# Unread products of TensorE at the end of the expert layers, and the key weights scaled there

## The chip, the cores and the metric

One core of one Trainium2 chip runs the whole program. The metric is the device time of one execution in microseconds, given as the median of three runs. Beside the runs stands one execution that was recorded by the profiler; all durations of single instructions come from it.

## What is computed

The reference runs two blocks of a network over 1024 tokens of width 1024 (the second block puts 16 learned tokens in front, so its first layer has 1040). What matters here is the second block. Its two layers each end in a mixture of 64 experts, and between the two lies latent attention:

```
h = h + short_conv_mixer(rmsnorm(h, ...))
h = h + hier_moe(rmsnorm(h, norm_ffn_g[0]), ...)      # experts, layer 0
a = rmsnorm(h, kv_g) @ w_dkv                          # key latents, 320 columns
cq = rmsnorm(rmsnorm(h, norm_mix_g[1]) @ w_dq, cq_g)  # query latents, 384 columns
... attention with 8 heads ...
h = h + hier_moe(rmsnorm(h, norm_ffn_g[1]), ...)      # experts, layer 1
return rmsnorm(h, final_norm_g)
```

`hier_moe` sends each token to two experts, multiplies their outputs by a gate and adds both to the token's row. All numbers are float32.

## The kernel before

The program is a chain of phases. A phase is a block in which each engine has its own instruction stream, and engines wait for each other through semaphores. At the end of a phase all five engines meet twice: first in the barrier that closes the block (L3363 for the experts, which is the line of `with nc.Block()`; L1924 for the phase ahead of them), then, after GpSimd has cleared the phase's semaphores, in a second barrier at L84. In the first one each engine runs a DRAIN instruction, raises a semaphore, and waits until GpSimd releases all.

`experts` runs twice, for layer 0 and for layer 1. It goes over 32 pairs of experts with weights that SyncE's queue loads three pairs ahead. For the last pair TensorE makes the products with the down weights in `down_half` (L3259); ScalarE and VectorE copy the result out of PSUM, and GpSimd scatters the rows to `ys` in HBM. SyncE waits for the scatters to land (L3403) and then issues the first loads of the next phase, `after.rows(sp)`. Ahead of that it has issued `after.start(sp)`: for layer 0 (`after` is a `LatentLoads`) the gains, the query weights `wq`, the key weights `wk` (L3638, issued at 1575.15 us) and rows of `h`. At the end of its stream ScalarE calls `after.scale_first`, which for layer 0 multiplies the query weights by the gains. A branch on `count` skips the part for experts with more than 64 rows; it is not run with these inputs. For layer 1 `after` is a `FinalLoads`, which only loads.

`combine_and_latents` (names beginning with `cl__`) follows layer 0. For each of nine tiles t of 128 tokens:

- `make(t)` on VectorE (L3606, L3607) adds the two gated expert rows to the row of `h`;
- `roots(t)` on ScalarE (L3848, L3850) takes the root of the mean square, and `scale(t)` on VectorE (L3911, L3915) divides by it;
- `turn(t)` on TensorE (L3766) transposes the tile, `turned_out(t)` on ScalarE (L3858) copies it out;
- `query_products(t)` (L3780) and `key_products(t)` (L3788) on TensorE multiply with `wq` and `wk`;
- ScalarE and VectorE normalise the latents, and TensorE turns them.

The order on each engine is written out by hand. VectorE: make(0), scale(0), make(1), the key weights times their gains (`pre.scale_second`, L3661, eight instructions), scale(1), make(2), scale(2), make(3), then a loop. ScalarE: roots(0), turned_out(0), roots(1), roots(2), roots(3), turned_out(1), and so on. TensorE: turn(0), query_products(0), turn(1), key_products(0), query_products(1).

`combine_out` (names beginning with `co__`) follows layer 1. It makes eight tiles of the output in the same way; VectorE adds the rows of five tiles and TensorE those of three (t = 2, 4, 6), VectorE scales all eight and SyncE stores them. The rows of tiles 0 to 3 are loaded by `after.rows` ahead of the barrier (L3999), those of tiles 4 to 7 behind it (L4034).

The phase ahead of the experts (`back_and_route`) already has unread products of TensorE:

```
def keep_busy(times):

    for i in range(times):
        mm(acc[:, A], ident[:], hnT[:, X[-1] % 2, 0:HK].rearrange("p k q -> p (k q)"), start=True, stop=True)
```

Its last instruction on TensorE is `keep_busy(6)` (L2205): six products of 128 by 128 with 128 by 512 elements that nobody reads, and then the barrier at L1924.

Of the kernel before, what the change touches and what calls it, by code (L numbers as in the profile page):

```python
# [11 lines left out]
P = 128  # L12
# [5 lines left out]
KT = DM // P  # L18
# [1788 lines left out]
QR = 384  # L1807
# [1345 lines left out]
def experts(nc, D, layer, tokens, keep, spill, gate, gu_slots, d_slots, xe, g_loaded, u_loaded, d_loaded, x_loaded, after, within):  # L3153
# [5 lines left out]
    with Phase(nc, "ex", within) as ph:  # L3159
# [121 lines left out]
        def y_second(b):  # L3281
            return nc.vector.tensor_copy(ysb[:, b, 512:], y_ps[:, 1])  # L3282
# [80 lines left out]
        with nc.Block() as block:  # L3363
# [87 lines left out]
            @block.tensor  # L3451
            def _(pe):

                def turn(p):
                    pe.wait_ge(x_loaded[p % 2], 16 * (p // 2 + 1))
                    if p >= 1:
                        pe.wait_ge(m["xT_out"], 2 * p)
                    turn_rows(p % 2).then_inc(m["x_turned"], 1)

                def last_product(p):  # L3460
                    pe.wait_ge(m["hT_out"], p + 1)
                    pe.wait_ge(d_loaded[p % RING], 16 * d_slots[p % RING].pieces * (p // RING + 1))
                    if p >= 1:
                        pe.wait_ge(m["y_out"], 2 * p)
                    down_products(p % 2, d_slots[p % RING].rows).then_inc(m["y_done"], 1)

                turn(0)
                for p in range(PAIRS_M):
                    end = p == PAIRS_M - 1
                    if end:  # L3470
                        last_product(p - 1)
                    pe.wait_ge(m["xT_out"], 2 * (p + 1))
                    pe.wait_ge(g_loaded[p % RING], 16 * (p // RING + 1))
                    gate_products(p % 2, gu_slots[p % RING]).then_inc(m["g_done"], 1)
                    if p >= 1 and not end:
                        last_product(p - 1)
                    pe.wait_ge(u_loaded[p % RING], 16 * (p // RING + 1))
                    up_products(p % 2, gu_slots[p % RING]).then_inc(m["h_done"], 1)
                    if p + 1 < PAIRS_M:
                        turn(p + 1)  # L3480
                    pe.wait_ge(m["h_out"], p + 1)
                    turn_hidden(p % 2).then_inc(m["h_turned"], 1)
                    if p == LOOK:
                        count = spilled(pe)
                pe.wait_ge(m["hT_out"], PAIRS_M)
                pe.wait_ge(m["y_out"], 2 * (PAIRS_M - 1))
                for k in range(2):
                    pe.wait_ge(d_ends[k], 16)
                    last = down_half((PAIRS_M - 1) % 2, d_slots[(PAIRS_M - 1) % RING].rows, k)
                last.then_inc(m["y_done"], 1)  # L3490
                with pe.If(0 < count):
                    spill_products(pe)
                    pe.wait_ge(m["y_out"], 2 * PAIRS_M)
                    for n in ("w_used", "x_used"):
                        pe.sem_inc(s[n], 1)
                    with pe.Fori(0, SPILL_PAIRS) as i:
                        with pe.If(2 * i < count):
                            pe.wait_ge(s["x_loaded"], 16 * i + 16)
                            turn_rows(0).then_inc(s["x_turned"], 1)
                            pe.wait_ge(s["xT_out"], 2 * i + 2)  # L3500
                            pe.wait_ge(s["gu_loaded"], 64 * i + 64)
                            gate_products(0, gu_slots[0]).then_inc(s["g_done"], 1)
                            up_products(0, gu_slots[0]).then_inc(s["h_done"], 1)
                            pe.wait_ge(s["h_out"], i + 1)
                            turn_hidden(0).then_inc(s["h_turned"], 1)
                            pe.wait_ge(s["hT_out"], i + 1)
                            pe.wait_ge(s["d_loaded"], 64 * i + 64)
                            down_products(0, d_slots[0].rows).then_inc(s["y_done"], 1)
                            pe.wait_ge(s["y_out"], 2 * i + 2)
                            for n in ("w_used", "x_used"):  # L3510
                                pe.sem_inc(s[n], 1)
# [47 lines left out]
            @block.vector  # L3559
            def _(dve):  # L3560
                v = Chain(dve, v_own)

                def rows_out(p):
                    dve.wait_ge(m["x_turned"], p + 1)
                    xT_second(p % 2).then_inc(m["xT_out"], 1)

                def y_half(p):
                    if p >= 2:
                        dve.wait_ge(y_stored[p % 2], 16 * (p // 2))
                    dve.wait_ge(m["y_done"], p + 1)  # L3570
                    y_second(p % 2).then_inc(m["y_out"], 1)

                rows_out(0)
                for p in range(PAIRS_M):
                    if p >= 1:
                        y_half(p - 1)
                    dve.wait_ge(m["silu_done"], p + 1)
                    dve.wait_ge(m["h_done"], p + 1)
                    hidden(p % 2).then_inc(m["h_out"], 1)
                    if p + 1 < PAIRS_M:  # L3580
                        rows_out(p + 1)
                    if p == 1:
                        gates(dve, v)
                    if p == 2:
                        spill_plan(dve, v)
                        dve.sem_inc(planned, 1)
                    if p == LOOK:
                        count = spilled(dve)
                y_half(PAIRS_M - 1)
                with dve.If(0 < count):  # L3590
                    spill_slots(dve, Chain(dve, slots_own))
                    with dve.Fori(0, SPILL_PAIRS) as i:
                        with dve.If(2 * i < count):
                            dve.wait_ge(s["x_turned"], i + 1)
                            xT_second(0).then_inc(s["xT_out"], 1)
                            dve.wait_ge(s["silu_done"], i + 1)
                            dve.wait_ge(s["h_done"], i + 1)
                            hidden(0).then_inc(s["h_out"], 1)
                            dve.wait_ge(s["seen"], i + 1)
                            dve.wait_ge(s["y_done"], i + 1)  # L3600
                            y_second(0).then_inc(s["y_out"], 1)


def gathered_sum(nc, v, y, gate, h, out, t):
# [87 lines left out]
def combine_and_latents(nc, D, gate, h_in, h_out, part, pre, cq, ckv, kr, next_loads):  # L3692

    QT, CT, KW = QR // P, KVR // P, KVR + ROPE
    with Phase(nc, "cl") as ph:
# [35 lines left out]
        with nc.Block() as block:  # L3731
# [24 lines left out]
            def _(pe):  # L3756
# [62 lines left out]
                def fold_parts(t):  # L3819
# [3 lines left out]
                    mm(aq[:, b, 0:QR], fold[:], parts[:, 0:QR], start=True, stop=True).then_inc(q_done, 1)  # L3823
                    mm(ak[:, b, 0:KW], fold[:], parts[:, QR:], start=True, stop=True).then_inc(k_done, 1)

                turn(0)
                for t in range(TT - 1):
                    query_products(t)
# [63 lines left out]
            def _(dve):  # L3892
# [53 lines left out]
                make(0)  # L3946
                scale(0)
                make(1)
                pre.scale_second(nc, dve)
                scale(1)  # L3950
                make(2)
                scale(2)
# [15 lines left out]
class FinalLoads:  # L3968
# [24 lines left out]
        sp.dma_start(self.hb[:, t], self.h_in[P * t:P * t + P]).then_inc(self.h_loaded[t], 16)  # L3993

    def scale_first(self, nc, act):
        pass

    def rows_in(self, sp, t):
# [320 lines left out]
```

## Time and profile before

| | us |
|---|---|
| median of 3 runs | 2768.99 |
| lowest and highest run | 2765.22, 2770.50 |
| the profiled execution: its own time | 2772.07 |
| the profiled execution: span from first to last instruction | 2770.4 |

The profiled execution took 1.67 us beside its span. Its mean granted TensorE clock was 0.971 of full speed. TensorE was busy for 2456.0 us of the span (89%), VectorE for 1064.8 (38%), ScalarE for 542.0 (20%), GpSimd for 345.0 (12%). A clock of 1.00 in a row is 2.4 GHz, 0.50 is 1.2 GHz. In the trace one float32 product of TensorE is two records (a weight load and a matmul each); a transpose is one.

### The profile page before, as it was taken

The numbers are of one execution on the slowest core, as the hardware profiler recorded it, in microseconds if no ns is written. First come the engines' busy times: TensorE is split into PE (matmuls) and PEld (weight loads), VectorE is DVE, ScalarE is ACT, GpSimd is POOL, SyncE is SP. The second block draws the span as 40 slices with busy tenths as digits, with TensorE's granted clock in tenths as the row PEclk, the third lists the DMA queues.
The fourth block names the chain that finished last, engine by engine and source line by source line (L and its number), as shares of the span: only waits on it lengthen the run. The fifth ranks groups of instructions, "written<-read, shape, count | busy, mean of one in ns | idle before, by whom it ended". The sixth has DMA issues, their size and how long they took to land. (4 is left out here: it accounts for less than half of the span.)

```text
span 2770.4 us, 39407 instructions
## 1 busy us (share of the span) xinstructions
PE 2456.0 (89%) x16286; PEld 1528.4 (55%) x16286; DVE 1064.8 (38%) x2180; ACT 542.0 (20%) x1226; POOL 345.0 (12%) x365
## 2 busy tenths in 40 slices
PE   9999988898999898997777779999999989787775
PEld 5444568447888554554444355766674545444442
DVE  3473654666555643211111153445545431111114
ACT  1312455210000011111111132322331111111112
POOL 3321002400000211111111000000003011111110
PEclk9999999999999999999999989999999999999998
DMA  3111010231113226999999970000113499999998
GB/s 117 35 38 52 6 48 5 83 110 46 32 45 119 99 107 254 416 425 425 425 426 426 395 296 23 17 25 8 49 48 137 178 379 424 425 426 425 426 424 331
DMA packets 86838, 566.06 MB, mean 204 GB/s; under 512 B 19312, under 2 KB 19472, under 8 KB 56688
## 3 DMA queue, kind: packets, MB, share of 16 engines
q1 hardware_dynamic: 61616, 506.86, 44.9%
q0 software_dynamic: 20144, 38.79, 3.7%
q10 hardware_dynamic: 4896, 17.83, 1.6%
q8 instruction: 133, 2.18, 0.3%
q14 instruction: 49, 0.40, 0.0%
HBM read 529.06 MB, written 65.01 MB: 214 GB/s over the span
## 5 line engine op out<-in xcount | busy, mean ns | idle before, releaser
L3231 PE MATMUL ex__h_ps<-all__arena,ex__xT 128*64 128x256 f32 x3392 | 407.7, 395 | 106.5 <-DMA all__arena<-in_w_up_t 82.2
L3231 PEld LDWEIGHTS ex__h_ps<-all__arena,ex__xT 128*64 128x64 f32 x3392 | 249.8, 142 | 276.5 <-DMA all__arena<-in_w_up_t 121.5
L3282 DVE COPY ex__ysb<-ex__y_ps 128x512 f32<-128x512 f32 x64 | 44.3, 692 | 495.8 <-PE ex__y_ps L3251 485.8
L3251 PE MATMUL ex__y_ps<-b__w,ex__hT 128*64 128x512 f32 x640 | 148.6, 606 | 30.5 <-issue 30.5
L3411 POOL DMA_INDIRECT b__rows<-s_hn,mo__queue x60 | 60.6, 1011 | 749.2 <-PE ex__x_ps L3224 749.2
L3273 DVE TENSOR_TENSOR ex__hs<-ex__sg,ex__h_ps 128x256 f32<-128x256 f32 x64 | 27.0, 422 | 304.5 <-PE ex__h_ps L3231 304.5
L2534 PE MATMUL cm__acc<-all__arena,cw__w 128*128 128x260 f32 x576 | 135.7, 386 | 2.6 <-PEq L84 2.3
L2534 PE MATMUL cm__acc<-all__arena,cm__sums 128*128 128x260 f32 x576 | 134.3, 383 | 0.2 <-DVEq L2610 0.2
L2534 PEld LDWEIGHTS cm__acc<-all__arena,cw__w 128*128 128x128 f32 x576 | 110.4, 192 | 20.4 <-issue 3.3
L2534 PEld LDWEIGHTS cm__acc<-all__arena,cm__sums 128*128 128x128 f32 x576 | 109.3, 190 | 17.4 <-issue 0.6
L3264 ACT COPY ex__xT<-ex__x_ps 128x512 f32<-128x512 f32 x64 | 37.5, 586 | 384.1 <-PE ex__x_ps L3224 384.1
L3251 PEld LDWEIGHTS ex__y_ps<-b__w,ex__hT 128*64 128x64 f32 x640 | 49.6, 139 | 109.4 <-issue 107.1
L2920 PE MATMUL hd__o<-all__arena 128*128 128x128 f32 x704 | 96.4, 282 | 6.4 <-ACT all__arena L2990 6.4
L2920 PEld LDWEIGHTS hd__o<-all__arena 128*128 128x128 f32 x704 | 85.0, 191 | 21.6 <-ACT all__arena L2990 14.9
L3231 PE MATMUL ex__h_ps<-mo__wx,ex__xT 128*64 128x256 f32 x704 | 80.8, 382 | 14.9 <-DMA mo__wx<-in_w_gate_t 7.8
L1955 POOL MEMSET mo__ident<- 128x128 f32 x2 | 0.4, 204 | 736.7 <-POOLq L84 736.7
L3279 ACT COPY ex__ysb<-ex__y_ps 128x512 f32<-128x512 f32 x64 | 37.5, 586 | 260.7 <-PE ex__y_ps L3251 253.0
L3224 PE MATMUL ex__x_ps<-mo__ident,b__rows 128*128 128x128 f32 x512 | 75.8, 292 | 13.6 <-PEq L84 13.6
L2075 PE MATMUL pb__acc<-b__w,all__arena 128*128 128x512 f32 x192 | 86.2, 593 | 1.8 <-PEq L84 1.8
L374 PE MATMUL fr__acc<-X__xT,fr__w 128*128 128x512 f32 x192 | 87.0, 603 | 0.0
L3224 PEld LDWEIGHTS ex__x_ps<-mo__ident,b__rows 128*128 128x128 f32 x512 | 63.3, 195 | 39.1 <-issue 39.1
L3416 POOL DMA_INDIRECT s_ys<-ex__ysb,mo__queue x64 | 64.4, 1006 | 108.7 <-DVE ex__ysb L3282 91.6
(546 smaller groups left out, 4088.8 us busy)
## 6 DMA issues: line engine op xcount, KB each, us to landing
all__arena<-in_w_up_t SPq DMA_DIRECT2D x64, 2048.0 KB, 43.7
all__arena<-in_w_gate_t SPq DMA_DIRECT2D x42, 2048.0 KB, 43.6
b__w<-in_w_down_t SPq DMA_DIRECT2D x40, 2048.0 KB, 44.8
mo__wx<-in_w_gate_t SPq DMA_DIRECT2D x22, 2048.0 KB, 43.7
all__arena<-in_w_down_t SPq DMA_DIRECT2D x22, 1024.0 KB, 36.9
mo__wx<-in_w_down_t SPq DMA_DIRECT2D x22, 1024.0 KB, 44.0
all__arena<-s_ys SPq DMA_DIRECT2D x15, 1024.0 KB, 11.2
cw__w<-in_conv_w_in_t SPq DMA_DIRECT2D x24, 512.0 KB, 4.5
```

Source lines behind the costliest of these rows:

```text
L374: last = mm(acc[:, bank], weight[:, k], moving(k), start=(first and k == 0), stop=(k == HKT - 1), skip_group_check=not first)
L2075: last = mm(acc[:, bank], weight[:, k], moving[:, k], start=(first and k == 0), stop=(last_here and k == HK - 1), skip_group_check=not first)
L2534: last = nc.tensor.matmul(bank(u, x), weight(k), moving(k, c), start=(k == 0), stop=(k == HK - 1))
L2920: last = mm(o_ps[:, h, 0:P], vv[:, s, h], pT[:, h, 4 * g + a], start=(g == 0 and a == 0), stop=(g == end and a == len(tiles_of(i)[g]) - 1))
L3224: last = nc.tensor.transpose(x_ps[:, k // 4, P * (k % 4):P * (k % 4) + P], xe[:, b, k::KT], ident[:])
L3231: last = nc.tensor.matmul(h_ps[half, c, DE * b:DE * b + DE], xT[:, b, k, half], slots[c][:, n, k], start=(k == 0), stop=(k == KT - 1))
L3251: last = nc.tensor.matmul(y_ps[half, c], hT[:, b, k, half], rows[k][:, n, 512 * c:512 * c + 512], start=(k == 0), stop=(k == 1))
L3264: return nc.scalar.copy(xT[:, b, 0:4].rearrange("p k q -> p (k q)"), x_ps[:, 0])
L3279: return nc.scalar.copy(ysb[:, b, 0:512], y_ps[:, 0])
L3282: return nc.vector.tensor_copy(ysb[:, b, 512:], y_ps[:, 1])
L3411: g.indirect_dma_start(xe[:, p % 2], None, hn_dram[:, :], bass.IndirectOffsetOnAxis(ap=queue[:, 0, p:p + 1], axis=0), bounds_check=T - 1, ...
L3416: g.indirect_dma_start(y_rows[:, :], bass.IndirectOffsetOnAxis(ap=queue[:, 1, p:p + 1], axis=0), ysb[:, p % 2], None, bounds_check=2 * T - ...
```

## The change

Three edits. At the end of TensorE's stream in `experts` stand 18 products of the identity with the first 512 columns of a buffer of gathered rows; nobody reads them, and the stream is that of both layers. In `combine_and_latents` TensorE makes six products of `wq` with itself ahead of turn(0), after a wait for the scaled query weights. And `scale_second` moves from VectorE's stream in `combine_and_latents` to the end of VectorE's stream in `experts` (for layer 1 the new method does nothing).

```
@@ experts, TensorE
                     last = down_half((PAIRS_M - 1) % 2, d_slots[(PAIRS_M - 1) % RING].rows, k)
                 last.then_inc(m["y_done"], 1)
+                for n in range(18):
+                    nc.tensor.matmul(x_ps[:, n % 2], ident[:], xe[:, 0, 0:512], start=True, stop=True)
                 with pe.If(0 < count):
@@ experts, VectorE
                             y_second(0).then_inc(s["y_out"], 1)
+                after.scale_second(nc, dve)
@@ combine_and_latents, TensorE
+                pe.wait_ge(q_scaled, KT)
+                for k in range(6):
+                    mm(aq[:, 1, 0:QR], wq[:, k, 0:P], wq[:, k], start=True, stop=True)
                 turn(0)
@@ combine_and_latents, VectorE
                 make(1)
-                pre.scale_second(nc, dve)
                 scale(1)
@@ FinalLoads
+    def scale_second(self, nc, dve):
+        pass
```

The place on TensorE at the end of the experts, the same in both layers (`ex__y_ps` takes the down products, `ex__x_ps` the new ones; L3353 is the part that the branch skips):

```order
 L3243 MATMUL ex__ht_ps<-mo__ident,ex__hs 128x128 x2
 L3259 MATMUL ex__y_ps<-b__w,ex__hT 64x512 x8
-L3491 COMPARE_AND_BRANCH
+L3492 MATMUL ex__x_ps<-b__rows,mo__ident 128x512 x18
+L3493 COMPARE_AND_BRANCH
 L3353 MATMUL ex__h_ps<-ex__hot_b,ex__hot_r 64x16 x36
```

The 18 products stand between the last down product and the branch that leads to the block's barrier.

The place on VectorE before, at the head of `combine_and_latents`:

```order
L3590 UNCONDITIONAL_BRANCH
L3891 UNCONDITIONAL_BRANCH
L3606 SCALAR_TENSOR_TENSOR all__arena<-all__arena,all__gate 128x1024
L3607 SCALAR_TENSOR_TENSOR all__arena<-all__arena,all__gate 128x1024
L3911 RECIPROCAL cl__rs<-cl__rt 128x1
L3915 TENSOR_SCALAR all__arena<-all__arena,cl__rs 128x1024
L3606 SCALAR_TENSOR_TENSOR all__arena<-all__arena,all__gate 128x1024
L3607 SCALAR_TENSOR_TENSOR all__arena<-all__arena,all__gate 128x1024
L3661 TENSOR_SCALAR all__arena<-all__arena,fw__gains 128x320 x8
L3911 RECIPROCAL cl__rs<-cl__rt 128x1
L3915 TENSOR_SCALAR all__arena<-all__arena,cl__rs 128x1024
```

And now, where the lines of the same calls are L3664, L3609, L3610, L3917 and L3921:

```order
L3592 UNCONDITIONAL_BRANCH
L3664 TENSOR_SCALAR all__arena<-all__arena,fw__gains 128x320 x8
L3363 UNCONDITIONAL_BRANCH
L3897 UNCONDITIONAL_BRANCH
L3609 SCALAR_TENSOR_TENSOR all__arena<-all__arena,all__gate 128x1024
L3610 SCALAR_TENSOR_TENSOR all__arena<-all__arena,all__gate 128x1024
L3917 RECIPROCAL cl__rs<-cl__rt 128x1
L3921 TENSOR_SCALAR all__arena<-all__arena,cl__rs 128x1024
L3609 SCALAR_TENSOR_TENSOR all__arena<-all__arena,all__gate 128x1024
L3610 SCALAR_TENSOR_TENSOR all__arena<-all__arena,all__gate 128x1024
L3917 RECIPROCAL cl__rs<-cl__rt 128x1
L3921 TENSOR_SCALAR all__arena<-all__arena,cl__rs 128x1024
```

The eight products of weights and gains stand ahead of the barrier (L3363), and between make(1) and scale(1) nothing is left.

TensorE at the head of `combine_and_latents`, now:

```order
L3493 UNCONDITIONAL_BRANCH
L3758 UNCONDITIONAL_BRANCH
L3831 MATMUL cl__aq<-all__arena 128x384 x6
L3769 MATMUL cl__tp<-cl__ident,all__arena 128x128 x8
L3783 MATMUL cl__aq<-all__arena 128x384 x8
L3769 MATMUL cl__tp<-cl__ident,all__arena 128x128 x8
L3791 MATMUL cl__ak<-all__arena 128x320 x8
```

Only the L3831 row is new there; L3769, L3783 and L3791 are L3766, L3780 and L3788 of before.

## Rows read from the trace of the kernel before

**Rows 1.** Windows: from:to, length, busy us by engine, granted clock, DMA share, GB/s.
```profile
1101.00:1620.00 519.00, 413.49 (x2921) 236.68 (x2921) 82.82 (x139) 72.58 (x153) 64.87 (x69) 0.96 1.00 416
1594.00:1605.80 11.80, 0.00 (x0) 0.00 (x0) 3.59 (x5) 3.18 (x6) 1.15 (x4) 0.50 0.83 326
```

**Rows 2.** Timeline of TensorE, end of layer 0's experts: start, length, what, idle before.
```profile
1585.86 3.65 PE L3259 MATMUL ex__y_ps<-b__w,ex__hT 128*64 128x512 f32 x16 [0.46 <-ACT ex__hT L3276]
1605.85 1.94 PE L3766 MATMUL cl__tp<-cl__ident,all__arena 128*128 128x128 f32 x8 [16.33 <-DVE all__arena L3915]
1608.89 8.12 PE L3780 MATMUL cl__aq<-all__arena 128*128 128x384 f32 x16 [1.10 <-ACT all__arena L3858]
1616.84 1.04 PE L3766 MATMUL cl__tp<-cl__ident,all__arena 128*128 128x128 f32 x8
1617.71 4.47 PE L3788 MATMUL cl__ak<-all__arena 128*128 128x320 f32 x16
1622.22 5.43 PE L3780 MATMUL cl__aq<-all__arena 128*128 128x384 f32 x16
```

**Rows 3.** Timeline of SyncE, VectorE and ScalarE, head of `combine_and_latents`.
```profile
1598.84 0.33 SPq L3736 DMA_DIRECT2D cl__cos<-in_cos_tok  x1
...
1600.54 1.28 DVE L3606 SCALAR_TENSOR_TENSOR all__arena<-all__arena,all__gate 128x1024 f32<-128x1024 f32 x1 [10.22 <-DMA all__arena<-s_ys]
...
1604.75 0.16 DVE L3911 RECIPROCAL cl__rs<-cl__rt 128x1 f32<-128x1 f32 x1 [1.60 <-ACT cl__rt L3850]
...
1608.44 2.46 DVE L3661 TENSOR_SCALAR all__arena<-all__arena,fw__gains 128x320 f32<-128x320 f32 x8 [0.23 <-DVE all__arena L3607]
...
1617.10 1.28 DVE L3606 SCALAR_TENSOR_TENSOR all__arena<-all__arena,all__gate 128x1024 f32<-128x1024 f32 x1 [0.27 <-DMA all__arena<-s_ys]
...
1621.18 0.99 ACT L3858 COPY all__arena<-cl__tp 128x1024 f32<-128x1024 f32 x1
```

**Rows 4.** The last tile's rows on the chain that ended last: start, length.
```profile
2738.19 18.73 DMA co__own_rows<-s_ys
```

**Rows 5.** The line of the experts' barrier, both layers: min/median/max ns, first to last start.
```profile
L3363 PEldq DRAIN  x2: 68/1465/2862, 1586.7 to 2727.7; - x2
...
L3363 SPq DRAIN  x2: 125/125/125, 1597.6 to 2735.4; - x2
```

**Rows 6.** The barrier ahead of layer 0's experts, in a window around it.
```profile
L1924 PEldq DRAIN  x1: 6080/6080/6080, 1087.9 to 1087.9; - x1
```

**Rows 7.** Timeline of TensorE there: unread products of `keep_busy`, five and six of them.
```profile
1078.51 4.50 PE L2205 MATMUL pb__acc<-pb__hnT,mo__ident 128*128 128x512 f32 x10
...
1088.62 5.37 PE L2205 MATMUL pb__acc<-pb__hnT,mo__ident 128*128 128x512 f32 x12
```

**Rows 8.** Timeline from the end of layer 1's experts to the last tile.
```profile
2721.61 3.65 PE L3259 MATMUL ex__y_ps<-b__w,ex__hT 128*64 128x512 f32 x16 [0.46 <-ACT ex__hT L3276]
...
2733.34 1.97 SPq L3999 DMA_DIRECT2D all__arena<-s_ys  x4
2736.87 1.28 SPq L4034 DMA_DIRECT2D all__arena<-s_ys  x3
...
2738.25 1.28 DVE L3606 SCALAR_TENSOR_TENSOR co__ho<-all__arena,all__gate 128x1024 f32<-128x1024 f32 x1 [12.19 <-DMA all__arena<-s_ys]
...
2740.95 1.06 ACT L4076 ACTIVATE co__sq<-co__ho 128x1024 bf16<-128x1024 f32 x1
2741.11 1.28 DVE L3606 SCALAR_TENSOR_TENSOR co__ho<-all__arena,all__gate 128x1024 f32<-128x1024 f32 x1 [0.25 <-DMA all__arena<-s_ys]
...
2746.07 1.28 DVE L3606 SCALAR_TENSOR_TENSOR co__ho<-all__arena,all__gate 128x1024 f32<-128x1024 f32 x1 [0.73 <-DMA all__arena<-s_ys]
...
2751.05 1.28 DVE L3606 SCALAR_TENSOR_TENSOR co__ho<-all__arena,all__gate 128x1024 f32<-128x1024 f32 x1 [0.74 <-DMA all__arena<-s_ys]
...
2757.02 1.28 DVE L3606 SCALAR_TENSOR_TENSOR co__ho<-co__own_rows,all__gate,all__arena 128x1024 f32<-128x1024 f32 x1 [0.33 <-DMA co__own_rows<-s_ys]
```

**Rows 9.** DMA issues by line: KB, us from issue to landing (key weights).
```profile
all__arena<-in_w_dkv_t SPq DMA_DIRECT2D x1, 1280.0 KB, 19.2
```

More of the change, by code:

```diff
@@ L3490, in _ @@
                 last.then_inc(m["y_done"], 1)
+                for n in range(18):
+                    nc.tensor.matmul(x_ps[:, n % 2], ident[:], xe[:, 0, 0:512], start=True, stop=True)
                 with pe.If(0 < count):
@@ L3601, in _ @@
                             y_second(0).then_inc(s["y_out"], 1)
+                after.scale_second(nc, dve)
 def gathered_sum(nc, v, y, gate, h, out, t):
@@ L3824, in fold_parts @@
                     mm(ak[:, b, 0:KW], fold[:], parts[:, QR:], start=True, stop=True).then_inc(k_done, 1)
+                pe.wait_ge(q_scaled, KT)
+                for k in range(6):
+                    mm(aq[:, 1, 0:QR], wq[:, k, 0:P], wq[:, k], start=True, stop=True)
                 turn(0)
@@ L3948, in _ @@
                 make(1)
-                pre.scale_second(nc, dve)
                 scale(1)
@@ L3995, in scale_first, with scale_second @@
     def scale_first(self, nc, act):
+        pass
+    def scale_second(self, nc, dve):
         pass
```

## The prediction

> **What bounds the kernel now.** I read the windows by stage first. The expert stages take more than a third of the span; the DMA engines are busy there for all of it, at 416 GB/s [rows 1]: weights bound them, and the change does not touch those. It touches the seam behind each. The timelines of the two seams come next, engine by engine, and there one asks which engine reaches the phase's barrier last, and whose work decides when the next steady stage begins.
>
> At the seam behind layer 0, TensorE ends its last product at 1589.5 and idles 16.3 us until turn(0) [rows 2]. Meanwhile the granted clock falls: 0.50, that is 1.2 GHz, from 1594 on [rows 1]. The last engine at the barrier is SyncE, whose DRAIN begins at 1597.6 and takes 0.125 us [rows 5]; the next phase starts at 1598.84, 1.1 us later [rows 3]. VectorE then waits for rows until 1600.54 and works through make(0) to make(3) [rows 3]. Query_products(1) starts at 1622.22, and two things are ready only then: TensorE, done with key_products(0) at 1622.18 [rows 2], and turned_out(1) on ScalarE, which begins at 1621.18 [rows 3] and stands behind roots(3) in ScalarE's order, so behind make(3) on VectorE. The two chains end together; this is what the change has to beat.
>
> At the seam behind layer 1, SyncE is last again (DRAIN at 2735.4 [rows 5]), and the phase starts at 2736.87 [rows 8], 1.35 us later. The chain that ended last runs from the load of the last tile's rows, 18.73 us in the queue [rows 4], over make of that tile at 2757.02 to the end.
>
> **The 18 products.** The nearest row is the same operation: `keep_busy(6)`, six products of this shape, is 12 records in 5.37 us; five are 10 records in 4.50 [rows 7]. So a record more costs 0.435 us. 18 products are 36 records: 5.37 + 24 x 0.435 = 15.8 us; I take 15.7, between this and 36 x 0.43. At layer 0 they start at 1589.3 (products are pipelined, so 0.2 before the end of the record) and end at 1605.0; at layer 1 the down products of 2721.61 and 3.65 us [rows 8] let them run from 2725.05 to 2740.75.
>
> Does the barrier wait for them? The same place at the earlier barrier says yes: TensorE's DRAIN there begins at 1087.9, takes 6.08 us and ends at 1093.98, just where the last unread product ends (1088.62 + 5.37 = 1093.99) [rows 6, 7]. The DRAIN of L3363 at layer 0 likewise ends at 1589.56, with the last product [rows 2, 5]. So TensorE becomes the last at the barrier in place of SyncE. No row has TensorE last at L3363, so the way from its arrival to the next start is bounded by the two seams with SyncE last, 1.1 and 1.35 us. Queued behind the products are only the branch and the barrier, but all other engines wait there.
>
> The Trainium skill (VectorE: DVE Perf Modes, section The DRAIN you can't avoid) tells of boilerplate DRAINs of about 12 ns, constant, on all engines. By that the products would not hold the barrier and the sum below would be about nothing; the 6.08 us in the trace stand against it here. The Trainium skill (TensorE: Matmul & The Clock Gate, section Back-to-back issue gap) gives 518 cycles for 512 columns, by which 18 products would take an estimated 3.9 us and end before SyncE arrives; the rows say four times that for this type.
>
> **Layer 0, the sum.** The phase starts at 1605.0 + 1.1 = 1606.1 in place of 1598.84. The rows of tiles 0 to 2, issued ahead of the barrier, have landed by then, so make(0) starts at once: 1606.15 for 1600.54, **+5.6**. The moved scaling takes 2.46 + 0.23 us out between make(1) and scale(1) [rows 3], but what it hid appears: scale(1) now waits for roots(1), as scale(0) does for roots(0), 1.60 us [rows 3]. With 0.1 of overlap that gives **-1.0**. The wait of make(3) for its rows, 0.27 [rows 3], goes as well: **-0.3**. (At the other bound those rows, asked for after make(0), land as late after it as before, and make(3) loses some 1.1; but the queue has by then emptied.) So turned_out(1) starts 5.6 - 1.0 - 0.3 = **4.3 us later**, and query_products(1) with it.
>
> TensorE gets its clock back: the transposes 1.94 to 1.04 us, the query products 8.12 to 5.43 [rows 2], 3.6 in all. It ends key_products(0) at 1622.2 + 5.6 - 3.6 = 1624.2. But query_products(1) can only start at 1626.5. The gain turns into an idle time of 2.3 us on TensorE. From there on TensorE runs without a gap, so 4.3 us is carried to the end.
>
> The six products in the new phase are 12 records of 384 columns at 5.43/16 = 0.34 us [rows 2], 4.1 us. They run while VectorE makes tile 0, the 5.3 us from the phase's start to turn(0); 1.2 us are to spare, and behind that the 2.3. Price: nothing. The scaling at its new place: the weights land 19.2 us after their issue [rows 9], at 1594.4; eight instructions later it is 1596.9, under the products that hold the barrier until 1605. Were it 8 us later it would count.
>
> **Layer 1, the sum.** The phase starts at 2740.75 + 1.25 = 2742.0 in place of 2736.87. make(0) begins at 2742.05 instead of 2738.25, where it waited for its rows: +3.8. VectorE waited four more times, 0.25, 0.73, 0.74 and 0.33 us [rows 8]; all these rows now lie ready: -2.05. ScalarE's first square comes 4.08 us after the phase's start [rows 8], as the tables are made first; scale(0) so waits about 0.2 more. **+1.9** at the last make and at the end. The rows of tiles 4 to 7 are asked for at 2742 instead of 2736.87, but the four ahead of them keep the queue busy: the fourth landed at 2746.07. The warm clock buys nothing here: TensorE waited for rows, and VectorE sets the end.
>
> **Sum: +6.2 us** (4.3 + 1.9). Bounds: 0.43 a record and 1.1 us for both barriers give 5.4; 1.35 for both and 0.435, 6.7; with late rows of tile 3, 7.8. On the profiled execution's 2772.07 it gives 2778.3. That execution lies 3.1 above the median of the runs; the terms are differences within it, so I put them on the median: 2769.0 + 6.2 = **2775.2**.
>
> **The rivals.**
> *The products don't hold the barrier* (not slower). Either the DRAIN passes them, or they take a quarter of the time. The point of decision is 1597.7, when SyncE arrives. VectorE then comes to make(3) 1.0 us earlier and waits for rows that landed at 1617.07; query_products(1) stays at 1622.2. 2769.0, at best 2768. For it speaks that a DRAIN with nothing queued is short (0.068 at layer 1 [rows 5]); against it rows 6 and 7. Chance 0.07.
> *VectorE catches up at the end.* If it finds more than the four waits to give back, the last rows' landing at 2756.9 sets the end as before: +4.3, 2773.3. The 2.05 counted speak against it. Chance 0.09.
> *The last rows starve.* Asked for 5.1 us later, they land later if the queue has run dry. It decides at 2746.07. The first row landed at most 4.9 us after its issue in an idle queue, 2733.34 to 2738.25 [rows 8], its own transfer included, so the fifth would begin well before. If not, the end moves by 5: 4.3 + 5.1 = 9.4, 2778.4. Chance 0.09.
> *TensorE, not VectorE, sets query_products(1).* Then layer 0 costs 2.0 and the whole 3.9: 2772.9. ScalarE's written order speaks against it. Chance 0.04.
>
> **How the numbers follow.** The forecast has 0.71; its own range, by the bounds and a spread of the runs, is 2773.5 to 2777.5. To leave out no more than 2 in 10 the range goes from 2771.5 to 2778.5. About 0.2%, 5.5 us, is what a measurement of this kernel can tell from no change: 2774.5. The forecast lies only 0.7 beyond, so of its 0.71 I give 0.46 to slower; with starving rows 0.55. Faster 0.03, the rest 0.42.
>
> **What would show it.** In the profile after: 36 records of the new line in some 15.7 us at each seam; TensorE's DRAIN at L3363 ending at about 1605 and 2740.7, last of the five; the phases starting 7 and 5 us later; the clock at 1.00 through both seams; transposes at 1.04 and query products at 5.4; an idle time of about 2.3 us of TensorE ahead of query_products(1), released by ScalarE; no wait for rows on VectorE. The prediction is wrong if the next phase starts near 1598.8, if the gap before query_products(1) is missing, or if the last make still waits for its rows.

## The result

The changed kernel takes 2777.97 us, the kernel before 2768.70 beside it on the same chip (medians of eight runs each). The ratio is 1.0030, with a 95% interval of 1.0021 to 1.0039: slower by 9.3 us, between 5.8 and 10.8. The forecast was 2775.2, slower by 6.2, with a range to 2778.5. One run of e1 and one of e3 below took far longer than all others of the same kernel (7456.25 and 2972.67 us); the ratios leave them out.

### The profile page after: what moved, and what is told of

The parts are those of the page before. It is cut to its first block and busy times, and to the rows that moved or that the text cites. A ratio compares the mean times of both kernels' runs of the same rounds, so it can differ in the third digit from the quotient of the medians.

```text
span 2776.1 us, 39575 instructions
## 1 busy us (share of the span) xinstructions
PE 2481.7 (89%) x16370; PEld 1542.5 (56%) x16370; DVE 1065.4 (38%) x2180; ACT 541.7 (20%) x1226; POOL 344.5 (12%) x365
```

## The profile after

The changed lines are L3492 (the 18 products), L3831 (the six products) and L3664 (the scaling). The others have moved: L3769, L3783 and L3791 are turn, query_products and key_products; L3609 and L3610 are make; L3739 issues the first load of the phase; L4042 asks for tiles 4 to 7 of the output.

TensorE's timeline from layer 0's last down products on: start, length, what, the idle time before and what ended it.

```profile
1584.15 3.65 PE L3259 MATMUL ex__y_ps<-b__w,ex__hT 128*64 128x512 f32 x16 [0.46 <-ACT ex__hT L3276]
1587.73 15.72 PE L3492 MATMUL ex__x_ps<-b__rows,mo__ident 128*128 128x512 f32 x36
1606.22 4.14 PE L3831 MATMUL cl__aq<-all__arena 128*128 128x384 f32 x12 [2.77 <-POOL cl__eps L3751]
1610.19 1.04 PE L3769 MATMUL cl__tp<-cl__ident,all__arena 128*128 128x128 f32 x8
1612.33 5.43 PE L3783 MATMUL cl__aq<-all__arena 128*128 128x384 f32 x16 [1.10 <-ACT all__arena L3864]
1617.60 1.04 PE L3769 MATMUL cl__tp<-cl__ident,all__arena 128*128 128x128 f32 x8
1618.47 4.47 PE L3791 MATMUL cl__ak<-all__arena 128*128 128x320 f32 x16
1625.01 7.12 PE L3783 MATMUL cl__aq<-all__arena 128*128 128x384 f32 x16 [2.07 <-ACT all__arena L3864]
...
1637.81 5.33 PE L3783 MATMUL cl__aq<-all__arena 128*128 128x384 f32 x16
```

The 36 new records take 15.72 us and end at 1603.45. Against [rows 2], turn(0) is down from 1.94 to 1.04 and query_products(0) from 8.12 to 5.43. But an idle time of 2.07 us, ended by ScalarE's copy of tile 1, now stands ahead of query_products(1), and that product takes 7.12 us, where it took 5.43 before.

The experts' barrier, both layers: duration in ns (min/median/max), first and last start.

```profile
L3363 SPq DRAIN  x2: 125/125/125, 1596.0 to 2739.1; - x2
L3363 PEldq DRAIN  x2: 1691/4577/7463, 1601.8 to 2736.3; - x2
```

The first row is SyncE, the second TensorE. In [rows 5] SyncE came last. It still comes at 1596.0 and 2739.1, but TensorE's DRAIN now lasts until the unread products have ended: 1601.8 + 1.69 = 1603.49 for products that end at 1603.45, and 2736.3 + 7.46 = 2743.76 for 2743.71.

The other engines at the head of `combine_and_latents`.

```profile
1604.55 0.33 SPq L3739 DMA_DIRECT2D cl__cos<-in_cos_tok  x1
1592.68 2.46 DVE L3664 TENSOR_SCALAR all__arena<-all__arena,fw__gains 128x320 f32<-128x320 f32 x8 [4.07 <-DMA all__arena<-in_w_dkv_t]
1604.69 1.28 DVE L3609 SCALAR_TENSOR_TENSOR all__arena<-all__arena,all__gate 128x1024 f32<-128x1024 f32 x1 [9.55 <-PEq L84]
1613.96 0.16 DVE L3917 RECIPROCAL cl__rs<-cl__rt 128x1 f32<-128x1 f32 x1 [1.60 <-ACT cl__rt L3856]
1623.97 0.99 ACT L3864 COPY all__arena<-cl__tp 128x1024 f32<-128x1024 f32 x1
1604.92 1.20 POOL L1392 TENSOR_SCALAR_AFFINE_SELECT cl__ident<-cl__ident 128x128 f32<-128x128 f32 x1 [0.15 <-POOL cl__ident L1390]
1606.08 0.09 POOL L3751 MEMSET cl__eps<- 128x1 f32 x1
```

The phase starts 1.10 us after the products' end. VectorE waits for the barrier (9.55 us) where in [rows 3] it waited for rows, and the scaling lies ahead of it. L3917 is scale(1), which now waits 1.60 us for roots(1). ScalarE's copy of tile 1 comes 1623.97 - 1584.15 = 39.82 us after the down products; in [rows 2, 3] it was 1621.18 - 1585.86 = 35.32.

The windows: from:to, length, busy us and instructions of TensorE, its weight loads, VectorE, ScalarE and GpSimd, granted clock, DMA share, GB/s.

```profile
1587.00:1604.00 17.00, 16.45 (x40) 6.76 (x36) 3.15 (x9) 4.63 (x9) 0.98 (x1) 1.00 0.71 279
1622.90:1625.00 2.10, 0.04 (x1) 0.00 (x0) 0.34 (x1) 2.07 (x5) 0.48 (x1) 1.00 1.05 439
1625.80:1629.20 3.40, 3.40 (x7) 1.86 (x6) 2.33 (x10) 0.69 (x4) 0.00 (x0) 0.50 1.00 407
1629.20:1632.00 2.80, 2.80 (x10) 1.55 (x10) 2.76 (x3) 0.00 (x0) 0.00 (x0) 1.00 0.65 272
```

The stretch that in [rows 1] had a clock of 0.50 is warm now. Behind the idle time the clock falls to 0.50, 1.2 GHz, for 3.4 us, inside query_products(1).

Layer 1's seam, answering to [rows 8].

```profile
2724.41 3.65 PE L3259 MATMUL ex__y_ps<-b__w,ex__hT 128*64 128x512 f32 x16 [0.46 <-ACT ex__hT L3276]
2727.99 15.72 PE L3492 MATMUL ex__x_ps<-b__rows,mo__ident 128*128 128x512 f32 x36
2745.12 1.27 SPq L4042 DMA_DIRECT2D all__arena<-s_ys  x3
2745.29 1.28 DVE L3609 SCALAR_TENSOR_TENSOR co__ho<-all__arena,all__gate 128x1024 f32<-128x1024 f32 x1 [16.42 <-PEq L84]
2745.49 1.23 POOL L1392 TENSOR_SCALAR_AFFINE_SELECT co__ident<-co__ident 128x128 f32<-128x128 f32 x1 [0.15 <-POOL co__ident L1390]
2750.09 1.04 ACT L4084 ACTIVATE co__sq<-co__ho 128x1024 bf16<-128x1024 f32 x1
2751.57 0.17 DVE L4103 RECIPROCAL co__rs<-co__rt 128x1 f32<-128x1 f32 x1 [0.85 <-ACT co__rt L4086]
2762.66 1.27 DVE L3609 SCALAR_TENSOR_TENSOR co__ho<-co__own_rows,all__gate,all__arena 128x1024 f32<-128x1024 f32 x1
```

The waits for rows are gone, the last make's too. New is a wait of 0.85 us at scale(0), for a square on ScalarE that comes 4.97 us after the phase's start (4.08 in [rows 8]). In the chain that ended last, [rows 4]'s load no longer stands:

```profile
DVE 1%; ACT 0%; issue 0%; POOL 0%; POOLq 0%; DVEq 0%; ACTq 0%
```

**Where the 9.3 us are.** I measure each seam from the start of its last down products, so that what happened earlier drops out. In layer 0 the landmark is query_products(2), since TensorE has no gap from there on in both traces: 1637.81 - 1584.15 = 53.66 us after, 47.46 before, +6.20. In layer 1 it is the last make: 38.25 after, 35.41 before, +2.84. Together 9.0. The two spans differ by only 5.7, because stretches outside these landmarks were shorter in the execution recorded of the changed kernel: layer 0's down products came 1.71 us earlier, and the stretch from query_products(2) to layer 1's down products was 1.69 shorter.

All landmarks, in us after the start of that layer's last down products, each the difference of two starts in that kernel's timeline. The phase start is SyncE's first issue behind the barrier.

| kernel | layer 0: phase start | query_products(1) | query_products(2) | layer 1: phase start | last make |
|---|---|---|---|---|---|
| before | 12.98 | 36.36 | 47.46 | 15.26 | 35.41 |
| changed | 20.40 | 40.86 | 53.66 | 20.71 | 38.25 |
| e1, scaling alone | 13.10 | 36.52 | 47.62 | 15.43 | 35.12 |
| e2, products in layer 0 alone | 20.40 | 42.04 | 53.14 | 15.35 | 35.92 |
| e3, nine products | 12.78 | 34.90 | 47.70 | 15.41 | 35.25 |
| e4, gap filled | 20.40 | 40.86 | 51.96 | 20.72 | 38.25 |
| e5, without the six | 20.41 | 41.29 | 52.39 | 20.72 | 38.26 |
| e6, ScalarE's order alone | 12.96 | 36.20 | 47.20 | 15.30 | 35.58 |
| e7, nine in layer 0 and the order | 13.23 | 32.51 | 43.51 | 15.32 | 35.27 |
| e8, 27 products | 28.13 | 48.60 | 61.39 | 28.44 | 45.98 |
| e9, VectorE waits for the constants | 20.41 | 42.07 | 53.17 | 20.72 | 38.11 |
| e10, scaling at its old place | 20.41 | 42.14 | 53.24 | 20.72 | 38.25 |

## The experiments

My theory: the products hold the barrier, and in each layer a part of that delay reaches the end. The first rival is that another part of the change costs.

**e1, the scaling alone.** The changed kernel without the 18 and without the six products; the scaling stays at the experts' end.

```
-                for n in range(18):
+                for n in range(0):
...
-                pe.wait_ge(q_scaled, KT)
-                for k in range(6):
-                    mm(aq[:, 1, 0:QR], wq[:, k, 0:P], wq[:, k], start=True, stop=True)
```

> The change without any unread product: only the scaling of the key weights stands at the end of VectorE's stream in the experts. Theory A (the 18 products hold the barrier of both layers, and the idle time ahead of query_products(1) brings the clock down): no cost is left; scale(1) comes about 1 us earlier, but make(3) then waits for its rows, so query_products(1) stays, 0 to -0.3 us: 2768.5. Theory B (a part of the loss is the moved scaling, which arrives late at the barrier or disturbs the copies there): 2 us or more above the kernel before, 2771 or later.

Measured: 2769.55 beside 2770.67, ratio 0.9994 (0.9985 to 1.0004). No difference, and the landmarks stand within 0.3 us of those of before. The cost lies with the products.

**e2, the products in layer 0 alone.**

```
-                for n in range(18):
+                for n in range(18 if layer == 0 else 0):
```

> The whole change, but the 18 products at the end of layer 0's experts alone. Theory A: layer 1's seam falls back by 2.8 us, layer 0's cost of 4.5 and the 1.7 of the slower clock stay: 6.2 us above the kernel before, 2774.9. The rival that the loads of the last rows set the end as before, so that layer 1's products cost nothing: as the changed kernel, 2778.

Measured: 2778.48 beside 2770.67, ratio 1.0026 (1.0017 to 1.0035), +7.8 us. Layer 0 carries the larger part: 5.68 by the landmark, while layer 1's is back near before (35.92 for 35.41). The time alone doesn't show layer 1's part: both expectations, 6.2 and 9.3 us above before, lie in its interval, and it overlaps that of the changed kernel. The landmarks show it. Its TensorE and VectorE also show something that the changed kernel's trace did not:

```profile
1608.42 5.58 PE L3831 MATMUL cl__aq<-all__arena 128*128 128x384 f32 x12 [2.77 <-POOL cl__eps L3751]
...
1617.33 0.16 DVE L3917 RECIPROCAL cl__rs<-cl__rt 128x1 f32<-128x1 f32 x1 [2.77 <-ACT cl__rt L3856]
...
1628.39 5.43 PE L3783 MATMUL cl__aq<-all__arena 128*128 128x384 f32 x16 [1.80 <-ACT all__arena L3864]
```

Here the six products, behind the same idle time of 2.77 us, took 5.58 us instead of 4.14. They hold turn(0) 1.45 us longer, ScalarE's copy of tile 0 with it, roots(1) behind that copy, and scale(1) waits 2.77 us instead of 1.60. Query_products(1) comes 1.18 later than in the changed kernel, but at full clock.

**e3, nine products in both layers.** Half as many, to end before SyncE reaches the barrier.

```
-                for n in range(18):
+                for n in range(9):
```

> 9 products in place of 18 in both layers: they end some 7.9 us after the last down product, SyncE arrives at the barrier some 8.3 us after it. Theory A: the barrier is not held, so the phases start as before. TensorE is done with key_products(0) some 3.6 us earlier, but query_products(1) starts as before: within 0.3 us of the kernel before, 2768.5; and if the longer idle time there brings the clock down again, 1.7 to 2.7 us more, 2770 to 2771. The rival that every product costs its share (half of the loss): 2773.3.

Measured: 2769.89 beside 2770.67, ratio 0.9999 (0.9990 to 1.0008). The nine take 7.99 us, the phases start within 0.2 us of before, and the time is that of before.

```profile
L3363 PEldq DRAIN  x2: 4566/5431/6296, 1590.8 to 2722.6; - x2
L3363 SPq DRAIN  x2: 125/125/125, 1595.4 to 2731.2; - x2
```

In layer 0 TensorE's DRAIN ends at 1590.8 + 4.57 = 1595.37, just as SyncE's begins; in layer 1 it ends at 2722.6 + 6.30 = 2728.90, 2.3 us ahead of SyncE's. In layer 0 query_products(1) begins 1.46 us earlier than before, and all of it is lost again in the product itself; the six products ahead of turn(0) are slow as well, behind an idle time of 1.96 us:

```profile
1597.34 5.83 PE L3831 MATMUL cl__aq<-all__arena 128*128 128x384 f32 x12 [1.96 <-POOL cl__eps L3751]
...
1618.71 7.12 PE L3783 MATMUL cl__aq<-all__arena 128*128 128x384 f32 x16 [2.39 <-ACT all__arena L3864]
```

**e8, 27 products.** Does each further record hold the barrier for its own length?

```
-                for n in range(18):
+                for n in range(27):
```

> 27 products in place of 18 at the end of each layer's experts, all else as in the changed kernel. If the barrier waits for TensorE to end the last product, each of the 18 further records (9 products, 0.43 us a record, 7.7 us) is a delay of the same length: the head of combine_and_latents comes 28.1 us after the start of the last down products where it came 20.40 with 18, query_products(2) at 61.4 us instead of 53.66, and in layer 1 the last make at 46.0 instead of 38.25; the time then is about 15 us above the changed kernel. If the barrier needs only that TensorE has taken the products into its queue, the head moves by less than half of that, and the time by less than 7 us.

Measured, in one execution: 2799.15, with 2770.71 for before beside it. Of these 28.4 us the landmarks hold 13.93 + 10.57 = 24.5. The rest, as with e9 and e10, lies outside the landmarks, and single executions differ there: layer 0's last down products, ahead of everything that the edits touch, begin between 1580.39 and 1590.53 us in the twelve profiles. So the landmarks are what I compare. TensorE, layer 0:

```profile
1587.43 3.65 PE L3259 MATMUL ex__y_ps<-b__w,ex__hT 128*64 128x512 f32 x16 [0.46 <-ACT ex__hT L3276]
1591.02 23.44 PE L3492 MATMUL ex__x_ps<-b__rows,mo__ident 128*128 128x512 f32 x54
...
1636.03 7.12 PE L3783 MATMUL cl__aq<-all__arena 128*128 128x384 f32 x16 [2.07 <-ACT all__arena L3864]
```

The 18 further records take 23.44 - 15.72 = 7.72 us, and every landmark behind them moves by 7.73: both phase starts, query_products(2), the last make. So the barrier waits for the end of the last product. The 2.07 us of idle time and the 7.12 us behind it come out the same.

**e4, the gap filled.** Three more unread products on TensorE ahead of query_products(1), so that it doesn't idle there.

```
                 for t in range(TT - 1):
+                    if t == 1:
+                        for k in range(3):
+                            mm(aq[:, 1, 0:QR], wq[:, k, 0:P], wq[:, k], start=True, stop=True)
                     query_products(t)
```

> The whole change, and three more unread products of 384 columns (1.9 us) on TensorE behind key_products(0), in the 2.07 us in which it waits for the second tile. Theory A: the clock stays at 1.00 there, query_products(1) takes 5.4 in place of 7.1 us: 1.7 us below the changed kernel, 2776.2. The rival that the clock falls there for another reason than the idle time: 2778, with query_products(1) at 7.1 us.

Measured: 2778.36 beside 2770.67, ratio 1.0025 (1.0014 to 1.0036). The timeline is plain: query_products(1) starts at the same place and takes 5.43 us again, and query_products(2) comes 1.70 earlier than in the changed kernel, 4.50 later than before.

```profile
1621.13 2.10 PE L3836 MATMUL cl__aq<-all__arena 128*128 128x384 f32 x6
1623.37 5.43 PE L3783 MATMUL cl__aq<-all__arena 128*128 128x384 f32 x16
```

By the landmarks e4 costs 4.50 + 2.84 = 7.3 us, and 7.7 are measured. Between e4 and the changed kernel the intervals overlap: the 1.70 us are shown by the trace, not by the time.

**e5, without the six products** (and without their wait).

```
-                pe.wait_ge(q_scaled, KT)
-                for k in range(6):
-                    mm(aq[:, 1, 0:QR], wq[:, k, 0:P], wq[:, k], start=True, stop=True)
                 turn(0)
```

> The change without the six products at the head of the next phase; the 18 stay. Theory A (VectorE's chain, 40.9 us after the start of the last down products, decides when query_products(1) can start): the clock falls in the idle time ahead of turn(0), TensorE ends key_products(0) some 6 us later than the kernel before, at 42.4 us, so query_products(1) starts 1.5 us later than in the changed kernel, but without an idle time ahead of it and so at full clock: query_products(2) at 53.5 us, as in the changed kernel (53.7); 2778. The rival that the warm clock is worth the 3.6 us that it saves on the first tile: query_products(2) 3.6 us later, at 57.3, 2781.5.

Measured: 2776.97 beside 2771.10, ratio 1.0022 (1.0012 to 1.0033). TensorE:

```profile
1611.60 1.94 PE L3769 MATMUL cl__tp<-cl__ident,all__arena 128*128 128x128 f32 x8 [6.54 <-DVE all__arena L3918]
1614.63 6.89 PE L3783 MATMUL cl__aq<-all__arena 128*128 128x384 f32 x16 [1.10 <-ACT all__arena L3861]
...
1627.04 5.43 PE L3783 MATMUL cl__aq<-all__arena 128*128 128x384 f32 x16 [0.33 <-ACT all__arena L3861]
```

The clock falls in the idle time ahead of turn(0) and is still down in turn(0) and at the start of query_products(0). There it costs little, since the slower products fill the time in which TensorE would wait for ScalarE: of the 2.07 us idle 0.33 are left, query_products(1) runs at full clock, and query_products(2) comes 1.27 us earlier than in the changed kernel, at 52.39 where 53.5 was expected: the clock came back sooner, and query_products(0) took 6.89 us, not the 8.12 of before. So the six products, in these traces, lose rather than gain; the times don't tell the two kernels apart.

**e9, VectorE waits for the constants.** In layer 1 GpSimd's select took 1.23 us instead of 0.29, and ScalarE's square was late. Is VectorE's make(0) beside it the cause?

```
                 v = Chain(dve, v_own)
+                dve.wait_ge(const_done, 3)
                 dve.wait_ge(g_loaded, 16)
```

> The changed kernel, in whose last phase VectorE waits for GpSimd's identity before its first make. GpSimd's select takes 1.23 us in the changed kernel and 0.29 in the kernel before. Theory A (it is slow because VectorE works at the same time): 0.29 us again, ScalarE's first square some 0.9 us earlier against the phase's start, the last make 0.3 to 0.5 us earlier, at 37.8 us after the start of the last down products. The rival that the select is slow because it stands behind a barrier that TensorE ends: 1.23 us as before, the last make later by VectorE's wait, at 39.5.

One execution, 2786.25 us (median of before beside it 2771.10). GpSimd, VectorE and ScalarE behind layer 1's barrier:

```profile
2753.70 0.29 POOL L1392 TENSOR_SCALAR_AFFINE_SELECT co__ident<-co__ident 128x128 f32<-128x128 f32 x1 [0.15 <-POOL co__ident L1390]
...
2754.07 1.28 DVE L3609 SCALAR_TENSOR_TENSOR co__ho<-all__arena,all__gate 128x1024 f32<-128x1024 f32 x1 [16.99 <-POOL co__eps L4051]
...
2757.35 1.04 ACT L4084 ACTIVATE co__sq<-co__ho 128x1024 bf16<-128x1024 f32 x1
```

The select takes 0.29 us again, the square comes 4.02 us after the phase's start (2753.33), and the wait at scale(0) is gone. But make(0) starts 0.58 us later, so the last make gains only 0.14. VectorE's work beside it makes the select long; the order of the two is worth almost nothing.

**e10, the scaling at its old place,** all else as changed.

```
-                after.scale_second(nc, dve)
...
                 make(1)
+                pre.scale_second(nc, dve)
                 scale(1)
```

> The changed kernel with the key weights scaled at their old place, between make(1) and scale(1) of combine_and_latents. The prediction gave the move -1.0 us: scale(1) then has to wait 1.60 us for roots(1), so the 2.69 us of the scaling cover that wait and cost 1.0 net. By that the copy of tile 1 on ScalarE (turned_out(1)) and with it query_products(1) come 1.0 us later than in the changed kernel, at about 41.9 us after the start of layer 0's last down products in place of 40.86, and the key products of tile 0 don't wait longer. The rival, that the move gives nothing beside the products since another wait takes its place, puts query_products(1) at 40.9 again. Layer 1's seam stays as in the changed kernel: the last make 38.25 us after its down products.

One execution, 2784.88 us, with 2764.81 for before beside it; of these 20.1 us the landmarks hold 5.78 + 2.84 = 8.6. Query_products(1) comes at 42.14, 1.28 after the changed kernel. That is near the 41.9 expected, but by luck, since it isn't the price of the scaling: in this execution the six products took 5.68 us, as in e2 and e9, where query_products(1) came at 42.04 and 42.07 with the scaling moved. Against those two the old place costs 0.1.

```profile
1620.06 0.16 DVE L3916 RECIPROCAL cl__rs<-cl__rt 128x1 f32<-128x1 f32 x1 [0.19 <-ACT cl__rt L3855]
```

The row says why: scale(1) waits 0.19 us here and 2.77 in e2. The scaling fills a wait that is there anyway. What the move is worth in an execution whose six products run at full clock this run doesn't show.

**e6, ScalarE's order alone.** The kernel before, with the copy of tile t + 1 ahead of roots(t + 3), so that the copy doesn't stand behind make(3).

```
-                    if t + 3 < TT:
-                        roots(t + 3)
                     if t + 1 < TT:
                         turned_out(t + 1)
...
+                    if t + 3 < TT:
+                        roots(t + 3)
                     latent_roots(t)
```

> The kernel before with one change of order on ScalarE alone: turned_out(t + 1) stands ahead of roots(t + 3). Theory A: in the kernel before TensorE is done with key_products(0) no earlier than turned_out(1) is ready, so nothing is won: within 0.3 us of the kernel before. The rival that ScalarE's order alone delays query_products(1): 1 us or more faster.

Measured: 2771.53 beside 2771.10, ratio 1.0004 (0.9995 to 1.0013): nothing. TensorE is then the one that comes last to query_products(1), at half clock as before.

**e7, nine products in layer 0 alone, and that order.** The changed kernel with nine products in place of 18 in layer 0, none in layer 1, and the order of e6; the six products and the moved scaling stay. Fewer products (e3, there in both layers) and the order (e6) each did nothing alone. Together they are the warm clock, without holding the barrier, and the order that lets TensorE use it.

```
-                for n in range(18):
+                for n in range(9 if layer == 0 else 0):
```

> 9 products in layer 0 alone, the six products, the moved scaling, and turned_out(t + 1) ahead of roots(t + 3) on ScalarE. Theory A: the barrier is not held, TensorE is warm, and query_products(1) no longer waits for make(3): it starts when key_products(0) ends, some 32.5 us after the start of the last down products in place of 36.4, without an idle time in which the clock could fall: 3 to 4 us below the kernel before. The rival that VectorE's chain still sets the second tile's end (query_products(2) at 47.5 us or later): no gain.

Measured: 2767.70 beside 2771.10, ratio 0.9991 (0.9982 to 1.0000). TensorE, layer 0:

```profile
1602.46 5.43 PE L3783 MATMUL cl__aq<-all__arena 128*128 128x384 f32 x16 [1.10 <-ACT all__arena L3864]
...
1612.90 5.32 PE L3783 MATMUL cl__aq<-all__arena 128*128 128x384 f32 x16
```

Query_products(1) follows key_products(0) without a gap, at full clock; query_products(2) comes 3.95 us earlier than before, and 3.4 are measured. The six products took 5.83 us here too, behind 2.40 us of idle time, but query_products(0) runs at full clock. It is the fastest version here, by less than the 0.2% that a measurement tells for certain.

## Why the prediction was right, and where its sizes were off

**The barrier.** Right. TensorE's DRAIN is last at both seams and ends with the products; e3 (nine: no delay) and e8 (7.72 us of products, 7.73 of delay) fix it from both sides. The rival that the products don't hold it falls. The DRAINs of about 12 ns in the Trainium skill (VectorE: DVE Perf Modes, section The DRAIN you can't avoid) are those of a program's preamble and postamble. TensorE's at the block's end is another: it lasted 7.46 us behind queued products. The products took 15.72 us (15.7 expected), and the way from there to the next start 1.10 and 1.41 us (1.1 and 1.25).

**Layer 0 up to query_products(1).** Right: +4.3 expected, +4.50 measured, of which make(0) has 5.86 (5.6 expected) and the scaling, roots and rows together -1.36 (-1.3). In the two traces it is -1.00 from make(1)'s end to scale(1) (2.61 us before, 1.61 now) and -0.36 at make(3), near the -1.0 and -0.3 of the sum. No run puts the scaling back with the six products at full clock (e10 had them slow). The idle time of TensorE was to be 2.3 us and was 2.07, ended by ScalarE: the rival that TensorE sets query_products(1) falls.

**Layer 0 from there on: the step that failed.** "From there on TensorE runs without a gap, so 4.3 us is carried to the end", together with "the clock at 1.00 through both seams". The prediction named the idle time and charged nothing for it. In the changed kernel the clock fell to 0.50 behind it, and query_products(1) took 7.12 us: +1.70, so +6.20 for layer 0. E4 takes away the idle time alone and gets 4.50.

**The six products: "price: nothing".** Wrong. The cover of 1.2 us was not there: TensorE waits for GpSimd's constants, the select took 0.29 us in the trace of before and 1.20 now, and with the short fill behind it (L3751) it lets the six start only 1.67 us after the phase's start, so that turn(0) follows right on their end. And they don't keep the clock reliably: of the six kernels with 18 or 27 products and the six, three (changed, e4, e8) ran them in 4.14 us, and three (e2, e9, e10) in 5.58 to 5.68, all behind 2.77 us of idle time; with nine products (e3, e7) they took 5.83. Where they were slow behind 18, query_products(1) came 1.2 later and query_products(2) lay at 53.14 to 53.24; where they were quick and the gap was left open, at 53.66 (e8: less its 7.73). Either way the clock falls once and costs 1.2 to 1.7 us. Without them (e5) it falls where it costs 0.43.

**Layer 1.** The mechanism was right, the size 0.9 short. make(0) came 4.24 later (3.8 expected: 0.16 more each for the products and the barrier, and 0.12 for VectorE's start); the four places with waits for rows gave 2.09 back (0.04, 0.81, 0.82 and 0.42; 2.05 expected; at the first, 0.22 of VectorE's wait for its own result stands where the rows' 0.25 stood); scale(0) lost 0.71 (0.86 between make(1)'s end and the reciprocal, 0.15 before), where 0.2 was expected. Together 2.86, and 2.84 are measured. The last term is GpSimd's select beside make(0), which puts off ScalarE's tables and its first square; e9 shows that cause. VectorE gave back hardly more than the waits counted, and the rows of tiles 4 to 7 were never late: those two rivals fall too.

**The sum.** 6.2 expected; 9.0 by the landmarks and 9.3 by the medians. What was missing is 1.7 for a clock that falls behind an idle time that the prediction itself had drawn, 0.9 in layer 1, and 0.2 in the way to query_products(1). The measured 9.3 lies above the sum's own bounds (6.7, and 7.8 with late rows; by its own terms the lower one is 5.6, not 5.4), and 2777.97 above the range taken from them, which ended at 2777.5. The stated range covers it since it was drawn wider, up to where the rival of the starving rows would lie (2778.4), and that rival did not come. So the direction and the held barrier were foreseen; that the time fell inside the range is partly luck.

## What to carry to other kernels

Unread products that keep TensorE's clock were work like any other at this barrier: to be free they had to end before the engine that comes last there anyway (nine here, not 18). What ends behind it holds the next phase back, and how much of it reaches the end depends on the waits that it takes the place of: of 18 products' 7.42 us of later start in layer 0, 4.50 reached query_products(1), and of 5.45 in layer 1, 2.84 the last make; of the nine further ones in e8, all did. The warm clock paid only where TensorE was the one waited for, so first take away the order that makes it wait (e7 against e3 and e6). When a faster engine ends in a new idle time, price what that idle time does to the clock of the next product too.

## What the runs showed of the hardware that was not expected

- The clock's level behind a short idle time differs between executions. Ahead of the six products, behind 2.77 us, it held in three profiles (changed, e4, e8) and fell in three (e2, e9, e10), though the code of layer 0 up to there differs only in the number of products (e8) and the place of the scaling on VectorE (e10); it also fell behind 1.96 (e3) and 2.40 us (e7). Ahead of query_products(1), behind 2.07 to 2.39 us, it fell in all three that had such a gap (changed, e3, e8); behind 1.80 it held in three (e2, e9, e10), all of which had fallen shortly before. What decides was not settled. The Trainium skill (TensorE: Matmul & The Clock Gate, section Part 1: The HAM clock gate) says that the clock's monitor runs free of the kernel's start, so that the number of slow products differs between runs of one kernel; these rows, one execution of each kernel, agree with that and don't prove it.
- GpSimd's 128 x 128 select takes 0.29 us alone and 1.20 to 1.23 us when VectorE's make starts 0.20 to 0.24 us ahead of it, in all profiles here. In layer 1 of the changed kernel it starts 0.20 us after the start of make(0)'s first instruction; that ends at 2746.57, and the select at 2746.72. The Trainium skill (SBUF — State Buffer, section SBUF: two separate sides) tells of a port pair that the two engines share and that the later one waits for; the rows fit that, and none here shows the port itself.
